# Full-height matmul shapes, a small first tile joined from halves, and a second block that begins by tiles of tokens

## The chip, the cores and the metric

The kernel runs on one NeuronCore of a Trainium2 chip. The metric is the device time of one execution in microseconds (us), taken several times; the median counts.

## What is computed

Two transformer-like blocks in float32 on one sequence of 256 tokens by 1024 channels. The reference, cut to what the change touches:

```python
h = rmsnorm(x, mix_pre_norm)                 # block one
u = h @ w_in                                 # z, xbc, dt (16 columns), ly, lx, gates
y_a = ssd_mixer(u_z, u_xbc, u_dt, ...)       # ends in an rms norm over 2 groups of 512
...
x = x + rmsnorm(merged @ w_out, mix_post_norm)
x = x + rmsnorm(ffn(rmsnorm(x, ffn_pre_norm)), ffn_post_norm)

h = rmsnorm(x, norm_pre)                     # block two
cols = h @ w_in_2                            # dn_qkv, dn_b and dn_a (4 + 4 columns), gm_uv, ...
mem_kv = rmsnorm(mem, norm_mem) @ w_mem_kv
y_a = deltanet(dn_qkv, dn_z, dn_b, dn_a)     # decays and betas come from the 8 columns
y_b = spatial gating(gelu(gm_uv), gm_z)
y_c = sliding window attention, 8 query heads of 64 channels on 2 key/value heads
y_m = attention on mem_kv
out = x + rmsnorm(sum over n of sigmoid(gate_n) * (y_n @ w_up_n) @ w_out_2)
```

## The kernel before

**Weights as a stream.** All large weights come as a list of chunks (`stream_list`, L41), cut into 260 units of 128 x 1024 floats. SyncE fetches each unit into one of five `t_raw` buffers (`sp_program`). ScalarE rounds it into `t_wh` (the high part, L1230), VectorE subtracts and writes `t_wl` (the low part, L1741); there are four pairs of them. TensorE then does three matmuls for each product in this fp32r form: high times high, high times low, low times high (`three`, L605 to L607, 256 moving columns, 24 matmuls for a unit; or `mm` at L610 with 512 moving columns, 12 for a unit, where tokens are the stationary side). The activations are kept in the same two parts, `t_hh` and `t_hl` (or `t_br` for both).

**Order.** Each engine's program is written out by hand, and a `Walk` object (L194) in each of them counts units and ticks. `walk.unit()` splits units up to three ahead, and `walk.ahead(q)` splits them up to unit q. A tick follows each unit (except in the chunks that are taken "together"), and side work, the lanes, is hung on tick numbers by `walk.until(t)`: softplus of dt, convolutions, the delta-rule inverse, both attentions. So adding or taking away ticks in the stream shifts every number behind it.

**The start.** The first chunk of the stream is `dt`: 128 columns of `w_in`, of which 16 are wanted. SyncE issues its unit first, then the parameters, then the input x in four quarters, the constants, four more units, the masks, and the block-diagonal weights. ScalarE makes the high part of x times `mix_pre_norm`, VectorE the low part, and TensorE runs the 24 matmuls of `dt` on these. Then come column sums of the squares of x (four tiles, on true f32 operands, so each matmul is two records in the profile), the chunk `xbc4`, the spreading of the norm over all partitions, `xbc5`, and `g0`, which is the first to need the normed h (`h_parts`, L1814). `dt`, `xbc4` and `xbc5` use the unnormed x; the norm is put in afterwards.

**The other sums.** Column sums of the same kind stand for the ssd norm (L794, 8 matmuls), and for the norm of the memory input, 8 matmuls, before `ps1`.

**Where block two begins.** After the feed-forward's last down chunk come `mk2` and `mk3` (four units of `w_mem_kv_2`, 512 moving columns), while ScalarE and VectorE run `token_norm("fpost", "pre2")` (L1277, L1861): two row norms for two tiles of 128 tokens. TensorE turns both scaled tiles within the last unit of `mk3` (`turn_rows`), the parts are made of 256 tokens at a time, and `dn_ba`, a chunk of 128 columns of which 8 are wanted, is the first to use them (`chunk_by_k`, L643), ahead of `dnq0` to `dnq5`, `vu`, `vv` and the rest.

**Sliding window attention** (`sw_lane`, L1015) does its scores on 64 partitions of keys and queries, and its value product on 64 columns of values, for each of the 8 heads:

```python
kt, q = SWK_[r, 0, :], SWQt[r, i, :]          # r = 64 partitions of this head
mm(PB[6][:, 0:384], identB[:, :], maskW[:, :], True, False)
mm(PB[6][:, 0:128], q[:, 0:128], kt[:, 0:128], False, True)
mm(PB[6][:, 128:384], q[:, 128:256], kt, False, True)
...
o = PB[6][r, :]
mm(o[:, 0:T], SWV_[:, 0, r], pt[:, 0:T], True, False)
mm(o[:, 128:T], SWV_[:, 1, r], pt[:, T:384], False, True)
```

## Time and profile before

| | |
|---|---|
| three runs | 869.59, 869.72, 871.77 us; median 869.72 |
| the profiled execution | 871.67 us, of which the span is 869.8 |
| TensorE matmul busy | 848.3 us, 98% of the span |
| VectorE, ScalarE, GpSimd busy | 72%, 59%, 9% |
| DMA | 149.21 MB, 172 GB/s on the mean |

The profile has one execution. A matmul's duration includes its way through the array, which overlaps the next one's, so the cost of a matmul in a stream is the distance between two starts, and that is what is counted below. A busy TensorE also hides a low clock; the granted clock stands in the profile's windows (1.00 is 2.4 GHz, 0.50 is 1.2 GHz).

### The profile page before, as it was taken

The numbers are of one execution on the slowest core, as the hardware profiler recorded it, in microseconds if no ns is written. First come the engines' busy times: TensorE is split into PE (matmuls) and PEld (weight loads), VectorE is DVE, ScalarE is ACT, GpSimd is POOL, SyncE is SP. The second block draws the span as 40 slices with busy tenths as digits, with TensorE's granted clock in tenths as the row PEclk, the third lists the DMA queues.
The fourth block names the chain that finished last, engine by engine and source line by source line (L and its number), as shares of the span: only waits on it lengthen the run. The fifth ranks groups of instructions, "written<-read, shape, count | busy, mean of one in ns | idle before, by whom it ended". The sixth has DMA issues, their size and how long they took to land.

```text
span 869.8 us, 14548 instructions
## 1 busy us (share of the span) xinstructions
PE 848.3 (98%) x5760; PEld 776.0 (89%) x5760; DVE 624.1 (72%) x1124; ACT 509.0 (59%) x826; POOL 78.4 (9%) x83
## 2 busy tenths in 40 slices
PE   5999999999999999999999999999999999999997
PEld 5999999899989999999998799899899887778885
DVE  6787987988868766666665979777555467775765
ACT  5655778665367755555656787554544445544453
POOL 0200001201020111111112100500000100000000
PEclk9999999999999999999999999999999999999999
DMA  9457443466454655555554463844322243365541
GB/s 342 140 190 286 160 140 119 150 211 256 155 199 150 238 188 194 174 182 202 176 194 169 146 198 124 308 147 146 97 98 97 98 145 122 125 213 191 196 145 49
DMA packets 40588, 149.21 MB, mean 172 GB/s; under 512 B 4524, under 2 KB 4680, under 8 KB 39880
## 3 DMA queue, kind: packets, MB, share of 16 engines
q1 hardware_dynamic: 40520, 148.27, 50.2%
q8 instruction: 46, 0.75, 0.3%
q14 instruction: 22, 0.18, 0.1%
HBM read 147.18 MB, written 1.08 MB: 170 GB/s over the span
## 4 chain that ended last, share of the span: by engine, by line
PE 87%; DVE 7%; ACT 3%; issue 2%; DMA 1%; SPq 0%; DVEq 0%; ACTq 0%
PE bank L610 39%; PE bank L605 16%; PE bank L607 15%; PE bank L606 15%; PE bank L613 2%; DVE t_wl L1741 2%; DVE t_arena L1756 1%; DVE t_arena L1746 1%; ACT t_arena L1235 1%; DVE t_x L1756 1%; ACT t_hh L1235 1%; DMA t_x<-in_xin 1%; ACT t_wh L1230 1%; DVE t_sm L1753 1%; ACT t_br L1235 0%
## 5 line engine op out<-in xcount | busy, mean ns | idle before, releaser
L1741 DVE TENSOR_TENSOR t_wl<-t_raw,t_wh 128x1024 fp32r<-128x1024 f32 x260 | 316.6, 1226 | 112.1 <-ACT t_wh L1230 111.0
L1230 ACT ACTIVATE t_wh<-t_raw 128x1024 fp32r<-128x1024 f32 x260 | 273.4, 1058 | 128.3 <-PE bank L610 60.6
L605 PE MATMUL bank<-t_hh,t_wh 128*128 128x256 f32 x1144 | 330.3, 289 | 2.9 <-DVE t_hl L1746 1.5
L607 PE MATMUL bank<-t_hh,t_wl 128*128 128x256 f32 x1144 | 323.5, 283 | 0.0
L606 PE MATMUL bank<-t_hl,t_wh 128*128 128x256 f32 x1144 | 323.5, 283 | 0.0
L605 PEld LDWEIGHTS bank<-t_hh,t_wh 128*128 128x128 f32 x1144 | 219.1, 192 | 6.8 <-issue 4.2
L606 PEld LDWEIGHTS bank<-t_hl,t_wh 128*128 128x128 f32 x1144 | 219.2, 192 | 0.8
L607 PEld LDWEIGHTS bank<-t_hh,t_wl 128*128 128x128 f32 x1144 | 219.1, 191 | 0.0
L610 PE MATMUL bank<-t_wh,t_br 128*128 128x512 f32 x384 | 123.5, 392 | 0.2 <-POOL t_br L2454 0.2
L1756 DVE SCALAR_TENSOR_TENSOR t_arena<-bank,t_par,t_arena 128x255 f32<-128x255 f32 (+2 forms) x184 | 75.2, 474 | 45.0 <-ACT t_arena L1235 44.7
L610 PE MATMUL bank<-t_wh,t_hh 128*128 128x512 f32 x224 | 91.9, 410 | 1.8 <-DVE t_wl L1741 1.8
L610 PE MATMUL bank<-t_wh,t_hl 128*128 128x512 f32 x224 | 88.3, 394 | 0.0
L610 PE MATMUL bank<-t_wl,t_hh 128*128 128x512 f32 x224 | 88.2, 394 | 0.0
L610 PEld LDWEIGHTS bank<-t_wh,t_br 128*128 128x128 f32 x384 | 72.2, 188 | 16.2 <-issue 1.6
L1235 ACT ACTIVATE t_arena<-bank 128x512 f32<-128x512 f32 (+4 forms) x75 | 42.2, 575 | 62.0 <-PE bank L610 35.5
L610 PE MATMUL bank<-t_wl,t_br 128*128 128x512 f32 x192 | 74.9, 390 | 0.0
L2454 POOL TENSOR_TENSOR t_br<-t_arena,t_br 128x256 fp32r<-128x256 f32 x30 | 34.5, 1154 | 307.5 <-ACT t_br L1235 307.5
L1235 ACT ACTIVATE t_arena<-bank,t_par 128x256 f32<-128x256 f32 x76 | 37.6, 547 | 39.3 <-PE bank L607 39.3
L610 PE MATMUL bank<-t_arena 128*128 128x128 f32 (+5 forms) x360 | 54.5, 298 | 0.8 <-DVE t_arena L1746 0.8
L610 PEld LDWEIGHTS bank<-t_wh,t_hh 128*128 128x128 f32 x224 | 42.5, 190 | 12.6 <-DVE t_wl L1741 2.5
L610 PEld LDWEIGHTS bank<-t_arena 128*128 128x128 f32 (+2 forms) x360 | 45.2, 185 | 6.8 <-issue 2.9
L610 PEld LDWEIGHTS bank<-t_wh,t_hl 128*128 128x128 f32 x224 | 42.5, 190 | 9.4
(154 smaller groups left out, 850.3 us busy)
## 6 DMA issues: line engine op xcount, KB each, us to landing
t_raw<-in_ws SPq DMA_DIRECT2D x260, 512.0 KB, 3.9
t_br<-decay SPq DMA_DIRECT2D x1, 2048.0 KB, 8.4
t_arena<-in_post SPq DMA_DIRECT2D x3, 512.0 KB, 4.9
t_arena<-gates SPq DMA_DIRECT2D x1, 1536.0 KB, 10.6
t_x<-in_xin SPq DMA_DIRECT2D x4, 256.0 KB, 5.9
t_bd<-in_bd SPq DMA_DIRECT2D x1, 1024.0 KB, 11.6
t_x<-in_xtok SPq DMA_DIRECT2D x1, 1024.0 KB, 5.8
t_arena<-in_mem SPq DMA_DIRECT2D x1, 1024.0 KB, 8.1
```

The source lines that it names most:

```text
L605: e.matmul(o, wh, xh, start=first, stop=False, skip_group_check=True)
L606: e.matmul(o, wh, xl, start=False, stop=False, skip_group_check=True)
L607: return e.matmul(o, wl, xh, start=False, stop=last, skip_group_check=True)
L610: return e.matmul(o, l, r, start=st, stop=sp, skip_group_check=True)
L613: return e.transpose(o, i, ident[0:i.shape[0], 0:i.shape[0]])
L1230: e.activation(WH[q % NS][:, :], RAW[q % NR][:, :], ACT.Copy, bias=0.0, scale=1.0).then_inc(*hi.now(q))
L1235: return e.activation(o, i, f, bias=bias, scale=scale)
L1741: e.tensor_tensor(WL[q % NS][:, :], RAW[q % NR][:, :], WH[q % NS][:, :].bitcast(F), SUB).then_inc(*lo.now(q))
L1746: return e.tensor_tensor(o, a, b, op)
L1753: return e.tensor_scalar(o, a, s1, s2, op0, op1)
L1756: return e.scalar_tensor_tensor(out=o, in0=a, scalar=s, in1=b, op0=op0, op1=op1)
L2454: return e.tensor_tensor(o, a, b, op)
```

## The change

- **dt** leaves the stream. Its 16 columns come with the pre-norm weights as a small transfer, `first` (128 x 136). High and low parts of the weights lie side by side in 32 columns, so 16 narrow matmuls (8 with 32, 8 with 16 stationary columns) do the work of 24; the two halves of the result are added by the small matmul that turned it before (`fold`). Ahead of it stand five matmuls on zeros, whose result nobody reads. The transfers are issued in another order: first, x, unit 0, constants, unit 1, parameters.
- **Norm sums**: VectorE adds the tiles up to one, so the column sums of x and of the memory take 2 matmuls in place of 8, those of the ssd norm 4 in place of 8. The first norm's root is taken by ScalarE, with one Newton step in place of three.
- **g0** is taken unit by unit, not by pairs of both units.
- **Block two** begins with the chunk `vu`, moved ahead of `dnq0`: its four units are held together and run for the first 128 tokens, then for the second, and norm, turning and parts are done by tiles of tokens (`second_norm`). Behind it `dn_ba` is a small tile in the manner of dt, from its own transfer `gates`.
- **Sliding window attention**: keys lie in a tile of 128 partitions with zeros in the other 64, and the value product writes all 128 rows, of which 64 are used.
- Tick numbers of the lanes of block two move by 4, from the delta-rule inverse on by 5.

The diff, cut to its core:

```diff
-    s.append(("dt", "w_in", rng(DTC, 128)))
...
-    s.append(("dn_ba", "w_in_2", rng(DNB, 128)))
+    for i in range(2):
+        s.append((f"vu{i}", "moving", ("w_in_2", i, rng(GMU, 512))))
...
-            fetch(0)
-            e.dma_start(parT[:, :], par).then_inc(s_par, 16)
+            e.dma_start(DTW, first).then_inc(s_first, 16)
             for i in range(4):
                 e.dma_start(X[:, 2 * i:2 * i + 2, :], xin[:, 2 * i:2 * i + 2, :]).then_inc(s_x[i], 16)
+            fetch(0)
             e.dma_start(conT[:, :], con).then_inc(s_con, 16)
-            for q in range(1, NR):
+            fetch(1)
+            e.dma_start(parT[:, :], par).then_inc(s_par, 16)
+            for q in range(2, NR):
                 fetch(q)
...
+            def turn_tile(tt):
+                e.wait_ge(*a_ns.of("scaled", "pre2", tt, 0))
+                e.wait_ge(*d_ns.of("scaled", "pre2", tt, 1))
...
+                for k in range(8):
+                    m = tr(PB[TILE_BANK[tt][k // 4]][:, 128 * (k % 4):128 * (k % 4) + 128], XS[:, tt, 128 * k:128 * k + 128])
...
-                    m = column_sums(3, 2 * g, [SSQ[:, 4 * g + k, :] for k in range(2)], g == 0, g == 1)
+                    m = column_sums(3, 2 * g, [SSQ[:, 4 * g, :]], g == 0, g == 1)
...
-                    kt, q = SWK_[r, 0, :], SWQt[r, i, :]
+                    kt, q = SWK2[:, a_, :], SWQt[:, i, :]
...
-                    o = PB[6][r, :]
-                    mm(o[:, 0:T], SWV_[:, 0, r], pt[:, 0:T], True, False)
-                    mm(o[:, 128:T], SWV_[:, 1, r], pt[:, T:384], False, True).then_inc(*p_sw.now("o", i, a_))
+                    mm(PB[6][:, 0:T], SWV_[:, 0, :], pt[:, 0:T], True, False)
+                    mm(PB[6][:, 128:T], SWV_[:, 1, :], pt[:, T:384], False, True).then_inc(*p_sw.now("o", i, a_))
...
-            chunk_by_k("dt", YBh, YBl, x_weighted)
-            e.wait_ge(s_con, 16)
-            norm_sums_first("mix", 7, SC0)
-            norm_sums_last("mix", 7, SC0)
-            chunk("xbc4", YBh, YBl)
+            e.wait_ge(*d_const.of("warm"))
+            for _ in range(5):
+                mm(PB[3][:, 0:T], SC1[:, 0, 0:128], SC1[:, 0, :])
+            e.wait_ge(*d_dt.of("w"))
+            for k in range(8):
+                e.wait_ge(*d_xw.of(k))
+                mm(PB[6][0:32, 0:T], DTS[:, k, :], YBh[:, k, :], k == 0, False)
+                m = mm(PB[6][0:16, 0:T], DTS[:, k, 0:16], YBl[:, k, :], False, k == 7)
+            m.then_inc(*p_dt.now("dt"))
+            chunk("xbc4", YBh, YBl, {(1, 0): mix_sums})
...
-            chunk_by_k("dn_ba", Hh, Hl, normed("pre2"))
+            turn_tile(1)
+            us = walk.four(4)
+            for tt in range(2):
+                for i, u in enumerate(us):
+                    if tt == 0:
+                        split_ready(u)
+                    e.wait_ge(*d_hl.of("pre2", tt, 2 * i + 1))
+                    m = turned(f"vu{i // 2}", u, 2 * i, Hh, Hl, i == 0, i == 3, (tt,))
...
+            e.wait_ge(*d_rw.of("w"))
+            e.wait_ge(*a_ev.of("free", "vu", 0))
+            for k in range(8):
+                mm(PB[6][0:16, 0:T], BAS[:, k, :], Hh[:, k, :], k == 0, False)
+                m = mm(PB[6][0:8, 0:T], BAS[:, k, 0:8], Hl[:, k, :], False, k == 7)
+            m.then_inc(*p_rw.now("ba"))
...
+            def second_norm(q):
...
+                walk.ahead(q + 2)
+                x_squares(post, pre, 1, 0)
+                x_squares(post, pre, 1, 1)
+                walk.ahead(q + 3)
+                scaled(pre, 0)
+                root(pre, 1, 1)
+                walk.ahead(q + 4)
+                scaled(pre, 1)
+                e.wait_ge(*p_ht.of(pre, 0))
+                tile_parts(0, range(6))
+                walk.ahead(q + 6)
...
+                tile_parts(1, range(8))
```

**How it moves VectorE's instructions at the start.** Before (names: `t_br` the parts of x, `t_wl` a unit's low part, `t_arena` here the squares or the normed h, `t_sm` small statistics, `t_hl` the low part of h; line numbers are those of each kernel):

```order
L1741 TENSOR_TENSOR t_wl<-t_raw,t_wh 128x1024 [waits s_split_hi]
L1756 SCALAR_TENSOR_TENSOR t_br<-t_x,t_par,t_br 128x256 [waits s_xw_hi] x8
L1746 TENSOR_TENSOR t_arena<-t_arena 128x512 [waits s_norm_square]
L1746 TENSOR_TENSOR t_arena<-t_arena 128x512 [waits s_norm_square,s_norm_add]
L1741 TENSOR_TENSOR t_wl<-t_raw,t_wh 128x1024 [waits s_split_hi] x3
L1753 TENSOR_SCALAR t_sm<-bank 128x2 [waits s_norm_sum]
```

Now:

```order
L1871 SCALAR_TENSOR_TENSOR t_br<-t_x,t_arena,t_br 128x256 [waits s_xw_hi] x8
L1856 TENSOR_TENSOR t_wl<-t_raw,t_wh 128x1024 [waits s_split_hi]
L1861 TENSOR_TENSOR t_arena<-t_arena 128x512 [waits s_norm_square]
L1861 TENSOR_TENSOR t_arena<-t_arena 128x512 [waits s_norm_square,s_norm_add]
L1861 TENSOR_TENSOR t_arena<-t_arena 128x512 [waits s_norm_add,s_norm_square]
L1861 TENSOR_TENSOR t_arena<-t_arena 128x256 [waits s_norm_add]
L1856 TENSOR_TENSOR t_wl<-t_raw,t_wh 128x1024 [waits s_split_hi]
L1868 TENSOR_SCALAR t_sm<-bank 128x2 [waits s_norm_sum]
```

The first split stands behind the parts of x, the second behind two more adds, and only two splits, not four, stand ahead of the norm's statistics.

**TensorE at the same place.** Before, the last matmuls of dt, the sums and the first of `xbc4`:

```order
L605 MATMUL bank<-t_br,t_wh 128x256 [waits s_xw_lo]
L606 MATMUL bank<-t_br,t_wh 128x256
L607 MATMUL bank<-t_br,t_wl 128x256
L610 MATMUL bank<-t_con,t_arena 128x1 [waits s_norm_add,s_con]
L610 MATMUL bank<-t_con,t_arena 128x1 x3
L610 MATMUL bank<-t_con,t_arena 128x1 [waits s_norm_square]
L610 MATMUL bank<-t_con,t_arena 128x1 x3
L605 MATMUL bank<-t_br,t_wh 128x256 [waits s_split_lo]
```

Now, from the program's start to the first of `xbc4`; the pair of narrow matmuls stands there eight times:

```order
L621 MATMUL bank<-t_arena 128x256 [waits s_const_dve]
L621 MATMUL bank<-t_arena 128x256 x4
L621 MATMUL bank<-t_br,t_wh 32x256 [waits s_xw_lo,s_dt_dve]
L621 MATMUL bank<-t_br,t_wh 16x256
...
L616 MATMUL bank<-t_br,t_wh 128x256 [waits s_split_lo]
```

The sums are two matmuls now, in the middle of `xbc4`.

**TensorE where block two begins.** Before, the end of `mk3` with both tiles turned, and the first of `dn_ba`:

```order
L613 MATMUL bank<-t_con,t_arena 128x128 [waits s_row_added,s_conv_taps,s_row_square,s_mem_lo,s_split_lo]
L613 MATMUL bank<-t_con,t_arena 128x128 x7
L610 MATMUL bank<-t_wh,t_hh 128x512
...
L613 MATMUL bank<-t_con,t_arena 128x128 [waits s_row_added,s_row_square]
L613 MATMUL bank<-t_con,t_arena 128x128 x7
L610 MATMUL bank<-t_wh,t_hh 128x512
...
L605 MATMUL bank<-t_hh,t_wh 128x256 [waits s_h_lo,s_conv_taps,s_split_lo]
```

Now, from the second tile's turning through the first token tile of `vu`, to the small tile:

```order
L624 MATMUL bank<-t_con,t_arena 128x128 [waits s_row_added,s_row_square]
L624 MATMUL bank<-t_con,t_arena 128x128 x7
L621 MATMUL bank<-t_wh,t_hh 128x512 [waits s_row_added,s_h_lo,s_split_lo]
...
L621 MATMUL bank<-t_wh,t_hh 128x512 [waits s_h_lo,s_split_lo]
...
L621 MATMUL bank<-t_hh,t_br 16x256 [waits s_evac_act,s_rows_dve]
L621 MATMUL bank<-t_hl,t_br 8x256
```

The second turning has moved behind the whole of `mk3`, and 48 matmuls of `vu` stand ahead of the 16 narrow ones that replace 24.

## Rows read from the trace of the kernel before

**Rows 1.** The page, part 1: busy time of each engine
```profile
PE 848.3 (98%) x5760; PEld 776.0 (89%) x5760; DVE 624.1 (72%) x1124; ACT 509.0 (59%) x826; POOL 78.4 (9%) x83
```
**Rows 2.** Who TensorE waited for: total us, times, longest
```profile
PE bank L610 <- DVE t_arena L1746: 1.1, 2, 0.8
```
**Rows 3.** TensorE in order of time, the start: start us, us, instruction
```profile
8.53 0.55 PE L605 MATMUL bank<-t_br,t_wh 128*128 128x256 f32 x1 [8.53 <-DVE t_br L1756]
...
13.29 1.92 PE L610 MATMUL bank<-t_con,t_arena 128*128 128x1 f32 x16 [0.25 <-DVE t_arena L1746]
15.07 0.53 PE L605 MATMUL bank<-t_br,t_wh 128*128 128x256 f32 x1
...
20.01 0.28 PE L606 MATMUL bank<-t_br,t_wh 128*128 128x256 f32 x1
20.13 0.28 PE L607 MATMUL bank<-t_br,t_wl 128*128 128x256 f32 x1
...
30.68 0.36 PE L605 MATMUL bank<-t_hh,t_wh 128*128 128x256 f32 x1 [1.50 <-DVE t_hl L1746]
```
**Rows 4.** Windows: stretch, busy PE, PEld, DVE, ACT, POOL, granted clock, DMA share, GB/s
```profile
16.00:17.00 1.00, 1.00 (x7) 1.00 (x6) 1.00 (x2) 0.77 (x1) 0.00 (x0) 0.50 0.98 410
```
**Rows 5.** ScalarE in order of time, the start
```profile
4.67 1.06 ACT L1230 ACTIVATE t_wh<-t_raw 128x1024 fp32r<-128x1024 f32 x1 [2.66 <-DMA t_raw<-in_ws]
7.36 3.30 ACT L1235 ACTIVATE t_br<-t_x,t_par 128x256 fp32r<-128x256 f32 x8 [1.64 <-DMA t_x<-in_xin]
10.56 2.17 ACT L1235 ACTIVATE t_arena<-t_x 128x512 f32<-128x512 f32 x4
```
**Rows 6.** VectorE in order of time, the start
```profile
27.08 1.23 DVE L1741 TENSOR_TENSOR t_wl<-t_raw,t_wh 128x1024 fp32r<-128x1024 f32 x1 [2.09 <-ACT t_wh L1230]
...
29.15 0.87 DVE L1756 SCALAR_TENSOR_TENSOR t_arena<-t_x,t_par,bank 128x256 f32<-128x256 f32 x2
```
**Rows 7.** DMA of the first 40 us: GB/s in 40 slices of 1 us
```profile
GB/s 0 29 184 344 312 244 338 384 421 391 344 377 410 420 432 442 410 389 430 406 397 418 352 352 340 221 225 266 29 143 303 86 0 0 0 0 0 74 315 152
```
**Rows 8.** TensorE in order of time: sums of the ssd norm
```profile
193.51 1.84 PE L610 MATMUL bank<-t_con,t_arena 128*128 128x1 f32 x16
195.22 0.36 PE L605 MATMUL bank<-t_br,t_wh 128*128 128x256 f32 x1
```
**Rows 9.** TensorE in order of time, where block two begins
```profile
486.80 0.39 PE L610 MATMUL bank<-t_wl,t_hh 128*128 128x512 f32 x1
487.03 0.39 PE L610 MATMUL bank<-t_wh,t_hl 128*128 128x512 f32 x1
489.24 0.53 PE L610 MATMUL bank<-t_wh,t_hh 128*128 128x512 f32 x1 [1.82 <-DVE t_wl L1741]
...
493.69 1.03 PE L613 MATMUL bank<-t_con,t_arena 128*128 128x128 f32 x8
...
498.53 0.35 PE L605 MATMUL bank<-t_hh,t_wh 128*128 128x256 f32 x1
```
**Rows 10.** The window 490 to 491 us, columns as in rows 4
```profile
490.00:491.00 1.00, 1.00 (x4) 0.81 (x3) 0.93 (x4) 0.97 (x2) 0.00 (x0) 0.50 0.79 205
```
**Rows 11.** ScalarE in order of time: the high parts of h for block two
```profile
497.02 3.03 ACT L1235 ACTIVATE t_hh<-bank,t_par 128x256 fp32r<-128x256 f32 x8 [1.86 <-PE bank L613]
```
**Rows 12.** TensorE in order of time: a score product on 64 partitions, then the stream
```profile
738.48 0.92 PE L610 MATMUL bank<-t_arena 64*128 64x128 f32 x4
...
739.33 0.50 PE L610 MATMUL bank<-t_wh,t_hh 128*128 128x512 f32 x1
```
**Rows 13.** The same for a value product on 64 columns
```profile
749.04 0.86 PE L610 MATMUL bank<-t_pw,t_arena 128*64 128x256 f32 x4
...
749.84 0.50 PE L610 MATMUL bank<-t_wh,t_br 128*128 128x512 f32 x1
```
**Rows 14.** The same for an ssd product of these column counts on the full array
```profile
67.46 0.82 PE L610 MATMUL bank<-t_arena 128*128 128x256 f32 x4
...
68.03 0.36 PE L605 MATMUL bank<-t_hh,t_wh 128*128 128x256 f32 x1
```

More of the change, by code:

```diff
@@ L326, in dn_bank, with build_program @@
     return 3 + (DN_AT[name] + 1) % 3
-def build_program(nc, ws, par, con, masks, bd, rows, swt, xin, xtok, min_, post, decay, gates2, out):
+def build_program(nc, first, gates, ws, par, con, masks, bd, rows, swt, xin, xtok, min_, post, decay, gates2, out):
     ctx = ExitStack()
@@ L641, in chunk, with chunk_by_units @@
                     walk.tick()
+            def chunk_by_units(name, xh, xl, x_ready):
+                b = BANK[name]
+                for j in range(2):
+                    q = walk.unit(NS - 1 - j)
+                    wh, wl = weights(q, 8)
+                    split_ready(q)
+                    if j == 0:
+                        bank_free(name)
+                    for k in range(8):
+                        if j == 0:
+                            x_ready(k)
+                        m = three(half(b, j), wh[:, k, :], wl[:, k, :], xh[:, k, :], xl[:, k, :], k == 0, k == 7)
+                    m.then_inc(*unit.now(q))
             def chunk_by_k(name, xh, xl, x_ready):
@@ L878, in dn_lane @@
                     m.then_inc(*p_dn.now("kk", h))
-                yield from walk.until(178)
+                yield from walk.until(182)
                 for hf in range(2):
@@ L955, in dn_lane @@
                         prods(f"o{hf}", hf, ET, U)
-                yield from walk.until(209)
+                yield from walk.until(214)
                 for i in range(2):
@@ L1523, in act_program @@
                     e.wait_ge(s_x[k // 2], 16)
-                act(YBh[:, k, :], X[:, k, :], ACT.Copy, scale=pc("mixpre", k)).then_inc(*a_xw.now(k))
+                act(YBh[:, k, :], X[:, k, :], ACT.Copy, scale=WMIX[:, k:k + 1]).then_inc(*a_xw.now(k))
+            split(0)
             for i in range(4):
                 act(SC0[:, 2 * i:2 * i + 2, :], X[:, 2 * i:2 * i + 2, :], ACT.Square).then_inc(*a_sq.now("mix", i))
-            walk.cols("dt", True)
-            walk.cols("xbc4")
-            walk.cols("xbc5")
+            split(1)
+            walk.split_to = 2
+            walk.unit(2)
+            e.wait_ge(*d_rs.of("mix", "v"))
+            act(NW[:, 2, 0:2], NW[:, 1, 0:2], ACT.Sqrt).then_inc(*a_sq.now("mix", "root"))
+            walk.tick()
+            e.wait_ge(*p_dt.of("dt"))
+            walk.unit(2)
+            walk.tick()
+            e.wait_ge(s_par, 16)
+            walk.unit()
+            walk.tick()
             h_parts("mix", SC1)
+            walk.unit()
+            walk.tick()
             def gates(i):
@@ L1630, in act_program @@
                 act(MV[:, tt, :], PB[BANK["mv", tt]][:, :], ACT.Copy).then_inc(*a_ev.now("free", "mv", tt))
-            walk.cols("dn_ba", True)
+            walk.four(4)
+            for tk in range(2):
+                e.wait_ge(*tokens_done("vu1", tk))
+                act(GU[:, tk, :], PB[BANK["vu", tk]][:, :], ACT.Gelu_apprx_tanh).then_inc(*a_ev.now("free", "vu", tk))
+                walk.ahead(FIRST["dnq0"] + 2)
             for i in range(6):
@@ L2043, in rows_lane @@
             def rows_lane():
-                yield from walk.until(151)
+                yield from walk.until(155)
                 x = bat[3]
@@ L2172, in dn_out_lane @@
             def dn_out_lane():
-                yield from walk.until(206)
+                yield from walk.until(211)
                 e.wait_ge(*a_dn.of("osq", 1))
@@ L2177, in dn_out_lane @@
                 newton("dno", NW, 8)
-                yield from walk.until(208)
+                yield from walk.until(213)
                 e.wait_ge(*d_rs.of("dno"))
@@ new lines, in dve_program @@
+            split(1)
+            walk.split_to = 2
+            o, v, r, t, h = NW[:, 0, 0:2], NW[:, 1, 0:2], NW[:, 2, 0:2], NW[:, 2, 2:4], NW[:, 1, 2:4]
+            e.wait_ge(*p_norm.of("mix", "sum"))
+            ts(v, PB[7][:, 0:2], 1.0 / 1024, MUL, EPS, ADD).then_inc(*d_rs.now("mix", "v"))
+            e.wait_ge(*d_rs.of("mix", "v"))
+            ts(h, v, -0.5, MUL).then_inc(*d_rs.now("mix", "half"))
+            walk.unit(2)
+            e.wait_ge(*a_sq.of("mix", "root"))
+            e.reciprocal(o, r).then_inc(*d_rs.now("mix", "guess"))
@@ L2284, in dve_program @@
+            e.wait_ge(*d_rs.last())
+            tt(t, o, o, MUL).then_inc(*d_rs.now("mix", "oo"))
+            e.wait_ge(*d_rs.last())
+            tt(t, t, h, MUL).then_inc(*d_rs.now("mix", "t"))
+            e.wait_ge(*d_rs.last())
+            stt(o, t, 1.5, o, ADD, MUL).then_inc(*d_rs.now("mix"))
+            walk.tick()
+            walk.unit(2)
+            walk.tick()
+            walk.unit(2)
+            walk.tick()
+            h_parts("mix", SC1, X, WMIX, 7)
             e.tensor_copy(ROWR, PB[7][:, 0:T]).then_inc(*d_const.now("row"))
-            walk.cols("xbc5")
@@ L2286, in dve_program @@
-            h_parts("mix", SC1, X, "mixpre", 7)
+            e.wait_ge(s_par, 16)
+            walk.unit()
+            walk.tick()
             ts(hbr, pc("br", 0, 8), 0.5, MUL)
```

307 lines of the change are left out of this document (198 added, 109 removed).

## The prediction

> **What bounds the kernel now.** I read the busy times first [rows 1]: TensorE's matmuls fill 848.3 of 869.8 us, VectorE is second with 72%. Then the list of TensorE's waits, because at 98% the question is what the other 2% are. They are few: 8.5 us until the first matmul, 1.5 us before `g0` [rows 3], 1.8 us in `mk3` [rows 9], 1.1 us in all for two waits on a small VectorE operation [rows 2]. So behind the first 31 us the kernel is a stream of matmuls, and a change counts if it takes matmul time out of it, or closes one of these holes.
>
> A matmul's price is the distance of two starts. With 256 moving columns it is 0.12 us at the full clock [rows 3], with 512 columns 0.23 us, from 486.80 to 487.03 [rows 9]. At a granted clock of 0.50 only 7 matmuls of 256 columns start in 1 us [rows 4]; with 512 columns it is about 0.43 [rows 10]. Both holes in which TensorE had little to do are followed by such a stretch: the column sums at 13.29 us, then 1.2 GHz from 15.07 to about 18.5; the wait at 487.26, then 1.2 GHz from 489.3 to 492.9.
>
> **The change, part by part.** The sum goes against the profiled execution, 871.67 us.
>
> *The start.* Before, `g0` begins at 30.68 and its 48 matmuls end at 30.68 + 5.76 = 36.4. The new start I lay out by the rows. The DMA queue has moved 0.57 MB by 4 us, 1.11 MB by 6, 1.8 MB by 8, then some 0.4 MB per us [rows 7]. Unit 0 alone (0.52 MB) landed at 4.67 [rows 5], 0.8 us behind the moment at which that much had moved; I keep this 0.8. Now first and x (1.12 MB together) come first: x is in at about 6.9 instead of 7.3 or later for its first quarter, the first quarter (0.33 MB) at about 4.3, unit 0 at 8.3, unit 1 at 10.6 (1.6 and 2.6 MB with the constants).
> - ScalarE's eight parts of x (3.30 us for all, [rows 5]) start with the first quarter, so they end at 7.7. The narrow matmuls of dt run in their shadow: 16 x 0.12 = 1.9 us, cost nothing, where 24 and the sums took 8.53 to 15.07.
> - Unit 0 is split at 8.3 + 1.06 [rows 5] + 1.23 [rows 6] = 10.6: there `xbc4` starts, against 15.07.
> - Its second unit waits for the squares (2.17 us, [rows 5]) and split 1 on ScalarE, and four adds and split 1 on VectorE: 14.3, while the first unit ends at 13.5, or at 15.0 if it starts at the low clock. Then two sums, 16 narrow records instead of which 4 are left, the second unit to 17.6, the spread 0.4, and `xbc5` (5.8) to 23.8.
> - h: VectorE has splits 3 and 4 to do until 19.6, then `h_parts`, 1.3 us for each pair (0.87 for two, [rows 6], and 0.43 for the low part): from 20 to 26. ScalarE's split of unit 5 is in its way until 21.3, as that unit comes behind the masks and the 1 MB of block-diagonal weights. So `g0`'s first unit, which now wants a new k every 0.36 us, ends at about 27.2, not 26.7, the second waits 0.5 us for split 5, and `g0` ends near 30.6.
>
> That is 5.8 us sooner. I take back 1.0 us, because VectorE then stands about 1.7 us further behind TensorE than before and was close to it already, and 0.6 us for a first unit at 1.2 GHz: the five matmuls on zeros may lift the clock by 5 us, but from 8 to 10.6 TensorE has nothing, and after the sparse stretch before 15.07 it fell. **Start: -4.2 us**, between -7.5 (no stall) and -2.0.
>
> *The sums.* Sixteen records of column sums took 195.22 - 193.51 = 1.71 us [rows 8], 0.107 each. The ssd norm loses 8, the memory norm 12: **-2.1 us**. All of it is on the path, since the stream is gapless on both sides. VectorE's added adds (0.7 and 0.4 us) lie in its 28% of free time; if that cover is gone they delay a split and cost up to 1.1 us each.
>
> *Block two.* The wait that ends at 489.24 is for the low split of `mk3`'s first unit. VectorE does this split behind the second tile's post-norm, in both kernels, so I expect this 1.8 us wait to stay. From 489.24 I count what follows without `vu` (48 x 0.23 = 11.0 us in both). Before: until `dnq0` at 501.6 (498.53 + 24 x 0.12 and small waits). Now: two units of `mk3` 2 x 2.75, two turnings 2 x 0.8, 16 narrow matmuls 1.9 and 0.35 for changing the array's shape (below), and 0.6 of waits in the first token tile of `vu`, in which TensorE needs two more k every 1.4 us while ScalarE and VectorE make them in pieces of 128 tokens. Eight pieces of 256 took ScalarE 3.03 us [rows 11], so 16 pieces of half the size cost between 3.0 (by width) and 6.1 (by count). That gives 489.24 + 9.9 = 499.2 at the full clock and 500.4 with the low stretch of before. **Block two: -1.2 us**; the ends are -2.5 and +2.0 (pieces at 0.38 us each, which the four splits must then wait for). Behind the last wait of the narrow tile stand all of `dnq0` to `dnq5`; what they need, unit 8 split, can be done by 506, four us ahead.
>
> *Sliding window attention.* A score product on 64 partitions takes 739.33 - 738.48 = 0.85 us [rows 12], a value product on 64 columns 0.80 [rows 13]; the ssd product with the same moving columns (256 and 128, four records) on the full array 0.57 [rows 14]. Most of what lies between is at the borders of the group, not in it. So each of 8 heads gives back 0.28 + 0.23, and up to 0.15 more before the group. **-4.6 us**, between -4.0 and -5.2. The Trainium skill says on this, in "TensorEngine Tiling (Array Packing)", Key Properties: "Mode switching requires drain: Changing tiling mode (not just tile) drains the TensorE"; the rows agree, and that narrow shapes carry a price at all hangs on it.
>
> *The rest.* Two small turnings become f32 matmuls on 32 and 16 partitions, four records for two: **+0.4 us**. The delta-rule chain gets one more tick of air, and its wait of 0.8 us [rows 2] may go: **-0.5**, from -0.8 to +1.0, as GpSimd also clears the padded keys in that stretch. Two more table loads fall to ScalarE, which is idle 41% of the time [rows 1].
>
> **Sum**: -4.2 - 2.1 - 1.2 - 4.6 + 0.4 - 0.5 = -12.2 us; 871.67 - 12.2 = 859.5 for an execution like the profiled one. That one is 1.95 us above the median of the three runs, so the median should be 857.5.
>
> **The rivals.** A measurement of this kernel can tell about 0.3% (2.6 us) from no change.
> 1. *The start gives next to nothing.* VectorE splits, adds, normalises and convolves in the first 60 us nearly without rest, and TensorE's earlier start turns into waits for splits behind `g0`; or the first quarter of x does not land earlier, as transfers of one queue share the engines. For it: DMA runs at its ceiling until 25 us [rows 7]. Against: the rows leave over 4 us between start and need. Time 857.5 + 4.2 = 861.7.
> 2. *Both holes close.* The clock stays up after 5 us and in block two, nothing stalls: 857.5 - 1.6 - 1.2 - 0.7 = 854.
> 3. *Full shapes give nothing.* If the weights' loading set the pace, 64 columns would have to be cheaper than 128, and the full value products would cost the same or more. Rows 13 and 14 speak against. Without the 4.6 us: 862.1. By the Trainium skill ("TensorE: Matmul & The Clock Gate", LDWEIGHTS) the loading time goes with the columns, P/1.2 ns, which makes four loads of 128 instead of 64 columns 0.21 us dearer, 1.7 us for 8 heads: that estimate would make the term +1.7, not -4.6, and the time 863.8. The trace has the durations of the products themselves, and they decide.
> 4. *Block two starves, and it gets slower.* ScalarE and VectorE make the pieces of a token tile and the splits in series, not beside each other: 16 x 0.38 [rows 11] and 16 x 0.40 in turns is 12.5 us, with three splits of 2.29 each between them 19.3, from 493.4 on. `vu` and the small tile would then end near 516, and the splits behind them two units later, 7 us behind the forecast; and the broken stream would run `vu`'s 48 matmuls at 0.43 instead of 0.23 [rows 10], 9.6 us more: 857.5 + 16.8 = 874.3. It decides when `vu` and the narrow tile together take 28 us instead of 13.5. Against it: both engines have separate buffers for each k, so they overlap as they do from 497 on.
> 5. *The change does little*: several of 1, 3 and a milder 4 together, within 2.6 us of 869.7.
>
> **How the numbers follow.** Forecast 0.62, rival 1 0.15, rival 2 0.12, rival 3 0.05, rival 4 0.03, rival 5 0.03. The range 852.5 to 862.0 takes in the forecast with its bounds and the rivals 1 and 2; some 0.15 is left out. Faster by over 0.3%: 0.62 + 0.15 + 0.12 + 0.05 = 0.94; within 0.3% 0.03; slower 0.03.
>
> **What the profile of the changed kernel would show.** `xbc4` starting at 10.6 and `g0` ending near 30.6; four and eight records of column sums with 0.45 and 0.9 us around them; score and value products 0.57 us from the first start to the stream; the same wait of 1.8 us in `mk3`; `vu` without waits of a microsecond. The prediction is wrong if VectorE's waits behind `g0` add up to more than 2 us, if the padded products take 0.8 us as before, or if a stretch of 1.2 GHz lies in `vu`.

## The result, and the profile after

The changed kernel takes 864.76 us in the median of four executions (864.38 to 866.08); the kernel before, run beside it, takes 870.55 us (869.59 to 871.77). The ratio is 0.9935, with a 95% interval from 0.9917 to 0.9954. The forecast was 857.5 us, and the range ended at 862.0: a gain is there, 5.8 us, but it is half of the 12.2 us forecast. The profiled execution took 864.38 us, its span is 862.6.

First the busy times, against [rows 1]:

```profile
PE 839.6 (97%) x5726; PEld 771.2 (89%) x5726; DVE 624.8 (72%) x1130; ACT 511.0 (59%) x839; POOL 78.7 (9%) x84
```

TensorE is busy 8.7 us less, and the span is 7.2 us shorter; so there is more waiting than before. Who TensorE waited for, against [rows 2]:

```profile
PE bank L616 <- DVE t_wl L1856: 4.2, 4, 2.5
PE bank L624 <- DVE t_arena L1861: 3.3, 2, 1.7
PE bank L621 <- DVE t_wl L1856: 2.3, 2, 1.7
PE bank L621 <- DVE t_arena L1861: 1.7, 1, 1.7
PE bank L621 <- DVE t_px L1871: 1.4, 1, 1.4
PE bank L621 <- DVE t_arena L2428: 1.2, 1, 1.2
PE bank L624 <- ACT t_arena L1295: 0.9, 1, 0.9
```

The first, third and sixth line are the start, `mk3` and waits for splits that the forecast had counted on in some form. The other four are new. In TensorE's order of time they are five instructions:

```profile
566.83 1.10 PE L621 MATMUL bank<-t_px,t_arena 128*128 128x256 f32 x4 [1.44 <-DVE t_px L1871]
635.68 0.65 PE L624 MATMUL bank<-t_con,t_arena 128*128 128x128 f32 x4 [0.87 <-ACT t_arena L1295]
661.21 1.25 PE L624 MATMUL bank<-t_con,t_arena 128*128 128x128 f32 x8 [1.66 <-DVE t_arena L1861]
683.22 1.16 PE L621 MATMUL bank<-t_arena 128*128 128x128 f32 x8 [1.72 <-DVE t_arena L1861]
755.12 0.66 PE L624 MATMUL bank<-t_con,t_arena 128*128 128x128 f32 x4 [1.61 <-DVE t_arena L1861]
```

The number in brackets is the wait ahead of the group: 7.3 us together. In the same stretch the kernel before had a single one, of 0.8 us [rows 2]; so 6.5 us of waiting are new. The first is the spatial gating product (tick 171 of `gm_xm_lane`); the other four are steps of the delta-rule chain (`dn_lane`): a turning inside the inverse, the turning for step 32, a product of step 64, and the turning of the output.

Where the rest went shows best in the start times of the same instruction in both traces:

| instruction | before | after | difference |
|---|---|---|---|
| first small matmul of ssd (128x16) | 48.06 | 43.88 | -4.18 |
| column sums of the ssd norm | 193.51 | 189.81 | -3.70 |
| the stream behind them | 195.22 | 190.62 | -4.60 |
| column sums of the memory norm | 222.09 | 217.50 | -4.59 |
| spreading of that norm | 229.63 | 223.70 | -5.93 |
| end of the wait in `mk3` | 489.24 | 483.13 | -6.11 |
| first turning of the delta-rule keys | 542.71 | 544.64 - 11.0 | -9.07 |
| last turnings, of the merged branches | 828.81 | 821.63 | -7.18 |

(The 11.0 us are `vu`, which now runs ahead of that turning; 48 matmuls of 0.23.) Up to the seventh row the change is 9.07 us ahead, more than the forecast's sum of these parts. Then come the eight sliding window heads, which should give another 4.6, and instead 1.9 us are lost. The difference of 6.5 us is what the new waits add up to.

The start, against [rows 3]:

```profile
1.21 4.63 PE L621 MATMUL bank<-t_arena 128*128 128x256 f32 x10 [1.21 <-DVE t_arena L2428]
6.03 3.13 PE L621 MATMUL bank<-t_br,t_wh 128*32 128x256 f32 x16 [0.18 <-DVE t_br L1871]
11.63 0.39 PE L616 MATMUL bank<-t_br,t_wh 128*128 128x256 f32 x1 [2.48 <-DVE t_wl L1856]
15.35 0.61 PE L621 MATMUL bank<-t_con,t_arena 128*128 128x1 f32 x4 [0.60 <-DVE t_wl L1856]
```

`xbc4` starts at 11.63. Unit 0 is the cause: ScalarE, idle until the transfer was there, could split it from 9.26 on, where the forecast had 8.3:

```profile
9.26 1.06 ACT L1290 ACTIVATE t_wh<-t_raw 128x1024 fp32r<-128x1024 f32 x1 [1.10 <-DMA t_raw<-in_ws]
```

Against [rows 8], the ssd norm's column sums:

```profile
189.81 0.95 PE L621 MATMUL bank<-t_con,t_arena 128*128 128x1 f32 x8
190.62 0.36 PE L616 MATMUL bank<-t_br,t_wh 128*128 128x256 f32 x1
```

They take 0.81 us in place of 1.71. The beginning of block two, against [rows 9], and the window that answers to [rows 10]:

```profile
483.13 0.50 PE L621 MATMUL bank<-t_wh,t_hh 128*128 128x512 f32 x1 [1.66 <-DVE t_wl L1856]
...
485.99 1.04 PE L624 MATMUL bank<-t_con,t_arena 128*128 128x128 f32 x8
...
489.64 1.03 PE L624 MATMUL bank<-t_con,t_arena 128*128 128x128 f32 x8
...
501.40 0.28 PE L621 MATMUL bank<-t_hh,t_br 128*16 128x256 f32 x1
...
503.25 0.28 PE L616 MATMUL bank<-t_hh,t_wh 128*128 128x256 f32 x1
```

```profile
484.00:485.00 1.00, 1.00 (x6) 0.83 (x5) 1.00 (x3) 1.00 (x3) 0.00 (x0) 1.00 0.88 270
```

From 483.13 on TensorE does not wait again until `dnq0` at 503.25, and the granted clock is 1.00 where it was 0.50. A value product and a score product, against [rows 12, 13]:

```profile
740.54 0.81 PE L621 MATMUL bank<-t_pw,t_arena 128*128 128x256 f32 x4
741.11 0.47 PE L621 MATMUL bank<-t_wh,t_br 128*128 128x512 f32 x1
...
744.11 0.82 PE L621 MATMUL bank<-t_arena 128*128 128x128 f32 x4
744.58 0.59 PE L621 MATMUL bank<-t_wh,t_hh 128*128 128x512 f32 x1
```

0.57 us for 0.80, and 0.47 for 0.85, from the group's first start to the stream's next.

### The profile page after: what moved, and what is told of

Read it like the earlier page. It is cut to its first block, busy times and chain, and to the rows that moved or that the text cites. A ratio compares the mean times of both kernels' runs of the same rounds, so it can differ in the third digit from the quotient of the medians.

```text
span 862.6 us, 14506 instructions
## 1 busy us (share of the span) xinstructions
PE 839.6 (97%) x5726; PEld 771.2 (89%) x5726; DVE 624.8 (72%) x1130; ACT 511.0 (59%) x839; POOL 78.7 (9%) x84
## 4 chain that ended last, share of the span: by engine, by line
PE 79%; DVE 11%; ACT 4%; issue 3%; DMA 2%; SPq 0%; DVEq 0%; ACTq 0%
PE bank L621 34%; PE bank L616 15%; PE bank L618 14%; PE bank L617 14%; DVE t_wl L1856 3%; PE bank L624 2%; DMA t_raw<-in_ws 2%; DVE t_arena L1861 1%; DVE t_arena L1871 1%; ACT t_wh L1290 1%; DVE t_sm L1868 1%; ACT t_arena L1295 1%; DVE t_x L1871 1%; ACT t_hh L1295 1%; DVE t_sm L1861 0%
## 5 line engine op out<-in xcount | busy, mean ns | idle before, releaser
L1295 ACT ACTIVATE t_arena<-bank 128x512 f32<-128x512 f32 (+5 forms) x76 | 42.7, 573 | 54.5 <-PE bank L621 35.4
L621 PE MATMUL bank<-t_arena 128*128 128x128 f32 (+4 forms) x370 | 58.4, 306 | 2.9 <-DVE t_arena L1861 1.7
L621 PEld LDWEIGHTS bank<-t_arena 128*128 128x128 f32 (+2 forms) x370 | 49.1, 190 | 8.4 <-DVE t_arena L1861 2.1
L621 PEld LDWEIGHTS bank<-t_wh,t_hh 128*128 128x128 f32 x224 | 42.1, 188 | 10.6 <-DVE t_wl L1856 2.3
```

Of the source, the lines that this page charges most:

```text
L621: return e.matmul(o, l, r, start=st, stop=sp, skip_group_check=True)
L1295: return e.activation(o, i, f, bias=bias, scale=scale)
```

## The experiments

Two explanations of the new waits are tried against each other. Theory A: the delta-rule steps were moved by 4 and 5 ticks while the memory attention, the spatial gating and the sliding window kept their numbers, so steps now fall on ticks at which VectorE or ScalarE is busy with a neighbour, or held by one. Theory B: the shorter groups took away the time in which VectorE and ScalarE used to finish.

**The shapes alone** (bef_full), on the kernel before:

```diff
-                    kt, q = SWK_[r, 0, :], SWQt[r, i, :]
+                    kt, q = SWK2[:, a_, :], SWQt[:, i, :]
...
-                    mm(o[:, 0:T], SWV_[:, 0, r], pt[:, 0:T], True, False)
+                    mm(PB[6][:, 0:T], SWV_[:, 0, :], pt[:, 0:T], True, False)
```

> The kernel before with the full shapes of sliding window attention alone. In the trace of the change each score group stands 0.64 us in the stream where it stood 1.11, each value group 0.57 instead of 0.88: 0.78 us a head, 6.2 us for eight. Theory A (the delta-rule chain, put 4 to 5 ticks later, now shares its ticks with the work of the other lanes, and TensorE waits for it): the shapes are not to blame, so here the whole 6.2 us come out, about 864.3 us against 870.5, and TensorE's waits between 540 and 770 us stay near 1.5 us. Theory B (every group that got shorter gave VectorE and ScalarE less time before the next tick, and their work came to light as waits): 2 to 3 us of gain, 867.5 to 868.5, and waits of 3 us and more between 540 and 770.

Measured: 866.19 us against 870.51, ratio 0.9958 (0.9943 to 0.9973), so 4.3 us, near the forecast's 4.6 and between the two expectations. The 6.2 us counted each head as if it stood alone; where another small group stands beside it, they share a border. In the two traces the stretch from the first turning of the delta-rule keys to the last turnings shrank by 4.8 us (286.1 to 281.3). One new wait of 0.4 us stands ahead of the turning of the delta rule's output.

**The change without them** (aft_narrow):

```diff
-                    kt, q = SWK2[:, a_, :], SWQt[:, i, :]
+                    kt, q = SWK2[r, a_, :], SWQt[r, i, :]
...
-                    mm(PB[6][:, 0:T], SWV_[:, 0, :], pt[:, 0:T], True, False)
+                    mm(o[:, 0:T], SWV_[:, 0, r], pt[:, 0:T], True, False)
```

> The change with the sliding window back on 64 partitions and 64 columns. Theory A: 6.2 us dearer, 864.8 + 6.2 = 871.0 us, and the five new waits (before the groups at 565, 635, 659, 681 and 753 us) stay at about 8 us in all. Theory B: the slower groups give the air back, so the waits shrink by 3 us or more and the time is 866 to 868. The first two waits lie before or at the start of the attention heads and should stay under both.

Measured: 869.41 us, 4.6 us above the change. Four of the five waits are as long as they were (1.48, 0.87, 1.66, 1.73); the fifth, at the turning of the output, falls from 1.61 to 0.64. So theory B explains 1.0 of the 7.3 us, and no more.

**The tick numbers alone** (bef_dnlate), on the kernel before; every number of `dn_lane` and `dn_out_lane` on all four engines, two of them:

```diff
-                yield from walk.until(178)
+                yield from walk.until(182)
...
-                    yield from walk.until(188 + 3 * n)
+                    yield from walk.until(193 + 3 * n)
```

> The kernel before with nothing changed but the tick numbers of the delta-rule lanes on all engines, later by 4 and from the inverse on by 5, as the change has them. Theory A: this alone brings the waits, 5 to 8 us in all, so 875.5 to 878.5 us against 870.5. Theory B: no change within 1 us, since every group is as long as before; a gain of up to 1 us is possible, as the delta-rule chain then starts further behind its inputs.

Measured: 878.82 us, 8.3 us slower than before (ratio 1.0103, 1.0087 to 1.0118). Its TensorE waits in the same order:

```profile
576.97 1.10 PE L610 MATMUL bank<-t_px,t_arena 128*128 128x256 f32 x4 [1.92 <-DVE t_px L1756]
646.21 0.66 PE L613 MATMUL bank<-t_con,t_arena 128*128 128x128 f32 x4 [0.87 <-ACT t_arena L1235]
672.47 1.25 PE L613 MATMUL bank<-t_con,t_arena 128*128 128x128 f32 x8 [1.66 <-DVE t_arena L1746]
695.23 1.16 PE L610 MATMUL bank<-t_arena 128*128 128x128 f32 x8 [1.73 <-DVE t_arena L1746]
769.11 0.66 PE L613 MATMUL bank<-t_con,t_arena 128*128 128x128 f32 x4 [0.63 <-DVE t_arena L1746]
```

These are the five waits of the change, instruction for instruction, the last one as short as without the full shapes. The old kernel gets 6.8 us of waits from the numbers alone, and its own wait of 0.8 us goes: theory A. The two traces differ by 7.5 us behind the memory norm's column sums, so 1.5 us of that is not waiting; what it is was not tried.

**How such a wait comes about.** Take the one at 661.21. In the change, ScalarE around it:

```profile
649.56 0.60 ACT L1295 ACTIVATE t_arena<-bank 128x512 f32<-128x512 f32 x1 [5.09 <-PE bank L621]
653.56 0.60 ACT L1295 ACTIVATE t_arena<-bank 128x512 f32<-128x512 f32 x1 [3.40 <-PE bank L621]
654.06 0.47 ACT L1574 ACTIVATE t_px<-bank,t_sm 128x256 f32<-128x256 f32 x1
```

and VectorE:

```profile
655.10 0.17 DVE L2381 RECIPROCAL t_sm<-t_sm 128x2 f32<-128x2 f32 x1 [3.77 <-ACT t_px L1574]
...
658.74 0.68 DVE L1871 SCALAR_TENSOR_TENSOR t_arena<-t_arena,bank 128x512 f32<-128x512 f32 x1
659.34 1.22 DVE L1856 TENSOR_TENSOR t_wl<-t_raw,t_wh 128x1024 fp32r<-128x1024 f32 x1
660.48 1.28 DVE L1861 TENSOR_TENSOR t_arena<-t_arena,bank 128x512 f32<-128x512 f32 x2
```

The softmax of the fourth memory head and the third level of the inverse both start at tick 191. On ScalarE the delta-rule copies stand first, and the second of them waits 3.40 us for a product that TensorE makes further on in its stream. Behind it stands the exponential, at 654.06, though VectorE had its maximum ready since 651.3. VectorE stands 3.77 us idle for that exponential, with the updates of the inverse behind it in its queue; they come at 660.48, and TensorE, at tick 193, waits for them. No engine is short of time here: each of the two engines works through its instructions in the written order, and the two orders hold each other up.

**Two groups one tick later** (aft_ret1), in the change:

```diff
-                    yield from walk.until(171 + gp)
+                    yield from walk.until(172 + gp)
...
-                yield from walk.until(214)
+                yield from walk.until(215)
```

> The change with two groups of TensorE one tick later: the two spatial gating products (ticks 172 and 173 instead of 171 and 172) and the two turnings of the delta rule's output (215 instead of 214, VectorE's last step behind them 216). These are the places of the waits at 564.8 us (1.75 us of the group is waiting) and at 753 us (1.9 us). Theory A, with the waits as local collisions, each of them mended by a tick of stream: both go, 864.8 - 3.6 = 861.2 us. Theory B, and any theory in which VectorE as a whole is behind: the waits turn up again one tick later, 864 to 865 us.

Measured: 861.38 us (ratio to before 0.9901). The waits at 566.83 and 755.12 are gone and none took their place; the other three stayed as they were (0.87, 1.66, 1.72).

**The chain apart from the softmaxes** (aft_v2), on top of it:

```diff
-                    yield from walk.until((187, 190, 192)[level])
+                    yield from walk.until((187, 191, 193)[level])
...
-                    yield from walk.until(193 + 3 * n)
+                    yield from walk.until(194 + 3 * n)
```

> aft_ret1 with every delta-rule step from tick 188 on one tick later on all engines (second level of the inverse at 189, third at 192, and so on; the output turned at 216). In the trace of aft_ret1 three waits are left on that chain: 0.9 us at 633.6 (ScalarE copies behind the softmax of the third memory head), 1.8 at 658.3 (both updates of the third level, VectorE held 3.8 us before by the softmax of the fourth head) and 1.9 at 680.1 (a masked product queued behind the branch's low parts). Theory A (local collisions): the shift separates the steps from tick 187 and 191, at which those softmaxes start, so the first two waits go; the third may stay: 861.4 - 2.7 = 858.7 us. Theory B (VectorE is behind as a whole): each wait turns up again at the next tick, 861 us; and if new collisions come with the sliding window heads (ticks 195, 199) 863 us.

Measured: 858.32 us (ratio 0.9857, 0.9842 to 0.9872), as theory A had it. Of the chain's waits one of 1.3 us is left, at 656.8 and for ScalarE; the one at a product of step 64 went too.

The masked tiles sooner (aft_v3), in VectorE's lane:

```diff
-                    yield from walk.until(194 + 3 * n)
+                    yield from walk.until(193 + 3 * n)
```

> aft_v2, and VectorE makes the two masked tiles for the steps 32 and 64 one tick sooner, right behind the updates that free their buffer, ahead of the branch's low parts. Theory A: the third wait (1.9 us) goes too: 858.7 - 1.9 = 856.8 us. Theory B: no change against aft_v2.

Measured: 858.74 us, no difference. What this edit was to remove had gone with the shift; the expected 1.9 us were a miss.

And the chain two ticks later (aft_v4):

```diff
-                    yield from walk.until((187, 191, 193)[level])
+                    yield from walk.until((187, 192, 194)[level])
```

> aft_v3 with the delta-rule steps from 188 on two ticks later instead of one. Theory A says that the place on the ticks decides and not the distance: the second level then begins at 190, the third at 193, the turning of step 32 at 195, where the softmax of a sliding window head starts, so one or two waits of 1 to 2 us should come back: 857 to 860 us. A theory by which the chain only lacks air says the same time as aft_v3 or less, 856 us.

Measured: **857.28 us**, ratio to before 0.9842 (0.9826 to 0.9857), the lowest median of all, though its interval overlaps those of the two runs ahead of it. Behind 500 us, where the change has 7.3 us of waits, these two are left:

```profile
665.80 0.34 PE L621 MATMUL bank<-t_maskW,t_identB 128*128 128x384 bf16 x1 [0.64 <-DVE t_arena L1871]
750.93 0.34 PE L621 MATMUL bank<-t_maskW,t_identB 128*128 128x384 bf16 x1 [0.27 <-DVE t_arena L1871]
```

The larger waits that I expected to come back did not, and the stretch from the first turning of the delta-rule keys to the last turnings took 269.3 us where aft_v2 and aft_v3 took 270.2. So the time lies where theory A had it, but its strict form, by which only the place on the ticks counts, missed the waits.

**The chain one tick sooner than in the change** (aft_dn4), 4 ticks everywhere:

```diff
-                    yield from walk.until(193 + 3 * n)
+                    yield from walk.until(192 + 3 * n)
```

> The change with the delta-rule steps from tick 185 on one tick sooner, so that the whole chain is 4 ticks later than before and not 5. By air alone (fewer ticks, more waiting) it should be slower, 866 to 868 us. By place (theory A) it depends on which softmax a step meets: the second level now starts at 187, together with the softmax of the third memory head, and the third level at 190, ahead of the fourth's at 191; one wait grows, one shrinks, 863 to 867 us. The two waits at ticks 171 and 214 are not touched by the first and kept by the second.

Measured: 869.24 us (ten executions, 868.02 to 872.69), above both expectations. There are four waits behind 500 us in place of five, but they add up to 8.7 us, and two are long:

```profile
666.06 2.08 PE L621 MATMUL bank<-t_arena 128*128 128x128 f32 x8 [3.61 <-DVE t_arena L1861]
759.05 0.66 PE L624 MATMUL bank<-t_con,t_arena 128*128 128x128 f32 x4 [3.01 <-DVE t_arena L1861]
```

The windows from 665 to 671 us and from 761 to 763 us show a clock of 0.50. So the fifth tick of the change is worth 4.5 us, where the forecast gave it 0.5; in the trace 1.4 us more of waiting, and for the rest the low clock behind the long waits is the likely cause, which no run took apart.

**The order of the second norm** (v4_mk3), on the fastest version; here VectorE's part:

```diff
-                post_added(post, 1)
                 walk.ahead(q + 2)
+                post_added(post, 1)
```

> aft_v4 with the order of the second norm changed: VectorE makes the low split of mk3's first unit ahead of adding the second tile's post-norm, and ScalarE makes the high split of mk3's second unit ahead of that tile's squares. The wait in mk3 is 1.64 us in aft_v4. If it is there because VectorE does the split behind those two operations (1.41 us), the split is done 1.1 to 1.4 us sooner and the wait falls to 0.3 to 0.6 us; the second tile's norm has 1.2 us of its own slack before its turning, but the low split of the second unit comes no sooner, so part may turn up there: 856 to 857 us against 857.3. If the wait hangs on the transfer of the unit or on the bank, the time does not move.

Measured: 858.11 us (856.89 to 858.76), no gain.

```profile
482.33 0.50 PE L621 MATMUL bank<-t_wh,t_hh 128*128 128x512 f32 x1 [0.65 <-DVE t_wl L1855]
486.13 1.09 PE L624 MATMUL bank<-t_con,t_arena 128*128 128x128 f32 x8 [0.78 <-DVE t_wl L1855]
```

The wait in `mk3` falls from 1.64 to 0.65 us, so it is the order of the splits and the norm that makes it; 0.78 us turn up 3 us later at the next split. What is left of it, 0.2 us, is less than the executions differ by.

**A longer wait in `mk3`** (aft_hold), in the change:

```diff
+                e.memset(ar(72, 2, T), 0.0)
                 walk.ahead(q + 2)
```

> The change with one more VectorE operation, a memset of 128 x 512, ahead of the low split of mk3's first unit. By the 0.27 us for 256 elements it takes about 0.55 us, so TensorE's wait grows from 1.66 to 2.2 us. In all five profiles of kernels with the new start of block two the clock stays at 1.00 behind that wait, and in all three with the old one (waits of 1.8 us) it falls to 0.50 for 3.5 us. If the length of the wait decides, the clock falls here too and the kernel is 0.55 + 1.5 to 2 us slower: 867 us. If something else in the old start did it, only the 0.55 us show, 865.3 us, and the windows from 482 to 490 us stay at 1.00.

Measured: 867.15 us (866.59 to 868.07), 2.4 us above the change.

```profile
483.73 0.50 PE L621 MATMUL bank<-t_wh,t_hh 128*128 128x512 f32 x1 [2.12 <-DVE t_wl L1856]
```

```profile
485.00:486.00 1.00, 1.00 (x4) 0.72 (x4) 1.00 (x2) 1.00 (x3) 0.00 (x0) 0.50 0.94 360
486.00:487.00 1.00, 1.00 (x4) 0.81 (x3) 0.89 (x6) 0.38 (x2) 0.00 (x0) 0.50 0.19 74
```

0.5 us more of waiting, and a stretch at 0.50 from 485 to 488 us is back. From the memory norm's sums to the delta-rule keys the trace is 2.1 us longer than that of the change, so some 1.6 us are the low clock. In this profile the longer wait brought the stretch back; that the length alone decides is not shown, and the last section has executions of the kernel before that speak against a fixed rule.

**The start with fewer and with more matmuls on zeros.** Without the five (aft_nowarm):

```diff
-            for _ in range(5):
-                mm(PB[3][:, 0:T], SC1[:, 0, 0:128], SC1[:, 0, :])
```

> The change without its five matmuls on zeros ahead of the small dt tile. In the trace of the change TensorE's granted clock is 1.00 in every window from 0 to 32 us, though it has nothing to do from 9.2 to 11.6 us; in aft_ret1, with the same start, it averages 0.83 from 10 to 20 us. If the five matmuls hold the clock up, then without them a stretch of 3 to 4 us at 0.50 follows, in dt or at the start of xbc4: up to 1.8 us dearer, 866.5 us. If they do nothing for it: 864.8 us within 0.5, and the clock between 10 and 20 us is low in some executions with them and without them.

Measured: 865.87 us (ratio to before 0.9942, 0.9924 to 0.9959), not told apart from the change's 0.9935. With four more behind the small tile, on the fastest version (v4_fill):

```diff
+            for _ in range(4):
+                mm(PB[3][:, 0:T], SC1[:, 0, 0:128], SC1[:, 0, :])
             chunk("xbc4", YBh, YBl, {(1, 0): mix_sums})
```

> aft_v4 with four more matmuls on zeros, behind the small dt tile, into a bank that nobody reads: they take 1.7 us at the full clock and fill most of the 2.1 to 2.9 us in which TensorE waits for the first split of xbc4. Four of the seven profiles with the new start show 3 to 7 us at 0.50 from 10 to 18 us, which puts the groups at 44 us up to 1.5 us later (45.05 against 43.5). If that idle time causes it, no execution shows it here, and the median falls by 0.5 to 1 us: 856.5. If the four matmuls themselves run at 0.50 they take 3.4 us and delay xbc4 by 0.5 to 1 us.

Measured: 857.59 us (856.57 to 859.07), no gain. TensorE's wait ahead of `xbc4` is 0.57 us there instead of 2.12, and the clock was full: the mean of a whole execution is 0.998 to 0.999 in all four, where aft_v4 has 0.995 and 0.996. But `xbc4` began at 11.65 in place of 11.38, and the ssd matmuls at 44 us stand no earlier. What the full clock gives in `xbc4` is lost again to the splits, which come no sooner: at 15.37 and 38.03 us TensorE waits 0.59 and 0.64 us for them, and aft_v4, at the low clock, has neither wait. That this is the whole reason was not tested by itself.

## Why the prediction was wrong

**The step that failed** is the one sentence on the delta rule: "The delta-rule chain gets one more tick of air, and its wait of 0.8 us [rows 2] may go: -0.5, from -0.8 to +1.0". I compared the chain with its own inputs, to which it has kept its distance or gained one tick. But the numbers of `gm_xm_lane` and `sw_lane` stood still, so against them the whole chain moved by 4 to 5 ticks. Measured: 6.5 us more of waiting than before in the changed kernel; with the numbers alone changed, 6.0 us more of waiting and 8.3 us more of time. The diff had it, while the list of the change says too much with "the lanes of block two": only the delta-rule lanes and the small `rows_lane` move. I costed it by the one wait that was there, not by laying the new order of ScalarE and VectorE beside the durations for ticks 187 to 193. Its bound of +1.0 rested on GpSimd alone, which none of the five waits has to do with. None of the rivals had this mechanism; rivals 1 and 3 came nearer in time (861.7, and 862.1 or 863.8 us), each for a reason that the runs rule out.

Of the three signs of being wrong the first was met: the waits for VectorE behind `g0` add up to 10.9 us, over the 2 us set. But it was badly set, as they are 4.4 us in the kernel before; four of those, of 0.3 to 0.7 us, are missing in the prediction's list of waits. The other two signs, padded products at 0.8 us and a low clock in `vu`, were not met.

- **Start, -4.2:** right in the sum (-4.18), by luck in the parts. `xbc4` began at 11.63, not 10.6, as unit 0 arrived 1 us later than forecast; this and 0.7 us of new waiting used up the 1.6 us that I had taken back for other reasons. The first unit did not run at 1.2 GHz in this execution; in another with the same start (aft_v3) it did, from 11 to 18 us, and the first ssd matmul stands at 45.17 there, 1.3 us later. A wait of 0.66 us at 38 us is VectorE's backlog, as forecast; the one of 0.36 us at 49 us stood in the kernel before too, at 53 us. Rival 1 is out.
- **Sums, -2.1:** right: -0.90 and -1.34. A wait for VectorE ahead of `pl0`, 0.32 us before, is 0.78 now; that its additional adds do this was not tried by itself.
- **Block two, -1.2:** it gave 3.1, beyond the better end of -2.5. No wait came in `vu`, where I had put 0.6; the wait in `mk3` stayed, with 1.66 for 1.82; and the clock stayed up, which is the 1.2 us of rival 2. The run with the longer wait makes it likely that these two belong together. The 1.2 us count against the profiled execution of the kernel before, and not against each one: nine of the 33 executions of that kernel in the experiments have a mean granted clock of 0.999, as the profile of the change, which has no low stretch before 860 us. They took 869.2 to 870.1 us, those at 0.994 or 0.995 took 871.1 to 872.3, and the profiled one has 0.995. So the 1.95 us that the forecast took off for the median are most likely low clock too, and rival 2 took its 2.8 us of clock off a median in which part of them was gone already.
- **Shapes, -4.6:** right: 4.3 alone, 4.6 as a part of the change. Rival 3 does not hold: full value products took 0.57 us in place of 0.80. The loading rule of the Trainium skill ("TensorE: Matmul & The Clock Gate", LDWEIGHTS) would have made the term +1.7. The trace agrees with it on the loads themselves, for one took 136 ns with 64 columns and 190 with 128, which is 0.22 us for the four of a product where the estimate was 0.21; but the loads do not set the pace here, and the group got shorter all the same (lines below). The rule on changing the tiling mode ("TensorEngine Tiling (Array Packing)", Key Properties) stands: what went away lies at the borders of the groups, and less of it where two small groups share one.
- **Fold tiles, +0.4:** 0.61 us in place of about 0.3 each, +0.6.

The weight loads of the value products (PEld is TensorE's loading of weights; behind the bar the busy time in us and the mean of one in ns), in the kernel before and in the change:

```profile
L610 PEld LDWEIGHTS bank<-t_pw,t_arena 128*64 128x64 f32 x32 | 3.7, 136 | 3.6 <-issue 2.3
L621 PEld LDWEIGHTS bank<-t_pw,t_arena 128*128 128x128 f32 x32 | 5.8, 190 | 0.8
```

In rival 4, 7 + 9.6 makes 16.6 us and not 16.8; nothing hangs on it.

The miss of 7.3 us in time is 6.4 us of gain that did not come (5.8 for 12.2) and 0.8 us by which the kernel before, run beside the change, was slower than the 869.72 that the forecast started from. Between the two profiles 7.3 of the 12.2 us came: the failed step is 7.0 us off (6.5 us more of waiting where 0.5 less was forecast), and block two gave 1.9 us more than forecast, which hid that much of it. Without the step the forecast is a gain of 11.7 us; the version in which the waits are retimed away gains 14.0 (871.27 to 857.28). So the other terms together were too small by some 2.3 us, most of it block two's.

## What to carry to other kernels

When side work hangs on tick numbers, moving one lane is a change to all the lanes whose numbers stay: for every tick that two of them now share, write down each in-order engine's queue and ask which instruction waits on another engine, and what stands behind it. Here a stream that was 98% busy took seven microseconds of such waits without any engine being short of time, and moving the late steps by one or two ticks gave them back (864.8 to 857.3 us); one tick the other way cost 4.5 us. After a change that takes matmul time out, run the kernel once more with the side work retimed before judging the change.

## What the runs showed of the chip that I had not expected

A wait of 1.64 to 1.67 us on TensorE in `mk3` left the granted clock at 1.00 in the nine profiles that have it (the change and its variants). A wait of 1.81 or 1.82 us (the kernel before and the two runs built on it) or of 2.12 us (the run with the memset) was followed by some 3.5 us at 0.50 (1.2 GHz) in all four profiles, and with the memset half a microsecond of waiting cost 2.4 us. But the nine executions of the kernel before with a mean clock of 0.999 can have had no such stretch, though their program is the same: a single stretch in the memset's profile brings the mean to 0.997 already. They have no trace, so whether their wait was shorter stays open. No sharp limit is shown.

At the start, kernels with the same code fell to 0.50 in some profiles and not in others, behind waits of 2.1 to 2.9 us ahead of `xbc4`; the run without the five matmuls on zeros fell too, and it made no difference in time that the runs can tell. Where four more such matmuls cut that wait to 0.57 us, the mean clock of all four executions is full to 0.998 or 0.999, and no time was gained.

A weight load of 128 columns took 190 ns and one of 64 took 136, and still the product with four of the longer loads took 0.23 us less of the stream (0.57 for 0.80).
